# When the second latent block's experts are chosen: one head per 16 picks from pick 105, each with its own exponential, in place of one head per 8 picks from pick 52

## The chip, the core and the metric

The kernel runs on one core of one Trainium2 chip. The metric is device time in microseconds for one launch; lower is better. A core has TensorE (PE, matmuls), VectorE (DVE), ScalarE (ACT), GpSimd (POOL) and SyncE (SP), each with its own instruction stream; they wait for one another through semaphores. Transfers between HBM and on-chip memory are issued by POOL, ACT or SP and run on 16 DMA engines that all of them share.

## The reference

Two layers (`DEPTH = 2`) of a hybrid backbone work on 128 context tokens and 256 latent tokens, all rows of 1024 floats. A layer is a modulation, four token mixers, an output projection and a norm, and then the part that matters here, a retrieval of experts (PEER):

```python
q = (x @ wq).reshape(T, PEER_HEADS, 2, PEER_KEY_DIM // 2)          # 8 heads, two halves
s1 = einsum('thd,nd->thn', q[:, :, 0], k1); s2 = ... q[:, :, 1], k2  # 128 scores each
v1, i1 = lax.top_k(s1, 16); v2, i2 = lax.top_k(s2, 16)
cand_s = v1[..., :, None] + v2[..., None, :]                        # 16 x 16 sums
top_s, pos = lax.top_k(cand_s, 16); idx = cand_i[pos]               # 16 experts per head
g = softmax(top_s)                                                  # over the 16 of a head
a = einsum('td,tkd->tk', x, u[idx])                                 # 128 rows of u per token
y = einsum('tk,tkd->td', g * gelu(a), v[idx])                       # 128 rows of v per token
```

So each token needs 8 heads x 16 experts = 128 rows of `u` and 128 rows of `v`, 4 KB each, at addresses that depend on the data.

## The kernel before

Tokens are cut into three blocks of 128: block 0 is the context, blocks 1 and 2 are the latent tokens. A layer has two stages: an even stage (block 0) and an odd stage (blocks 1 and 2, which share attention). Over the whole kernel the experts are worked off as one line of 6 x 128 = 768 picks: a pick is one expert for each of a block's 128 tokens. The order is layer 0 blocks 0, 1, 2 and then layer 1 blocks 0, 1, 2; `BASE = [0, 128, 384, 512, 768]` (L49) is the pick at which each stage's experts begin. So stage 1 holds picks 128 to 383 (its second block from 256 on), stage 3 picks 512 to 767 (its second block from 640 on).

For a pick n the engines do this:
- POOL gathers 128 rows of `u` (L423) into slot n mod 4 of `u_rows` and, four picks later, the 128 rows of `v` (L430) into slot n mod 4 of `v_rows`. A gather of `u` waits until the row slot is free (the dot of pick n - 4 is done) and, at every 16th pick, for the head's indices (`idx_ready`); a gather of `v` waits until TensorE has added pick n - 4. POOL does u(n), v(n - 4), u(n + 1), v(n - 3), ... in that fixed order.
- DVE multiplies the rows with the token and sums (`dot`, L982).
- Every four picks ACT takes the gelu of four dots (L701), DVE multiplies by the softmax weight (`weigh`, L990), and ACT makes four diagonal matrices (L707).
- PE adds diagonal x rows into the block's result (`add`, L1302).

All other work (projections, attention, norms, the choice of the experts themselves) is laid beside this line by hand. Every piece carries a due pick, and `Beside` emits it on its engine behind the line's own instruction of that pick. DVE's dots run six picks ahead of its due picks (`DOT_AHEAD = 6`, L54): a piece due at pick t stands behind the dot of pick t + 6.

Choosing a head's experts has two steps. `best_eight` and `next_eight` find the 16 best of each half from the scores in PSUM; for an odd stage they do so for both blocks at once, in `late(s)`, one head per 16 picks: head h from pick BASE + 16h - 22 on, with two 8-matmul groups of the query projection on PE (L1079, one 1 MB `q_tile` load per head). `pick` (L752 to L778) then makes the 16 x 16 sums of one block and one head, takes the best 16, and writes 16 indices; it comes in three chunks, due at three picks one after another. It also writes the scores less their maximum to `gw`; ACT takes the exponential (`weights_exp`, L528) and DVE divides by the sum (`shares`, L803). For the first block of a stage `late` calls `pick` for each head, and each head has its own exponential. For the second block `second(s)` calls it (s = 1 and 3).

When a block's 128 picks are done, `update` (L956) adds the result to the tokens and norms them. Stage 2's token mixer (layer 1, block 0) is laid over picks 262 to 348, that is over the second block of stage 1. Layer 1's modulation weights (24 tiles of 1 MB, `ring`) run over picks 134 to 254. Over the second block of stage 3, picks 640 to 767, nothing is laid but its own line and the update of block 1 at 640.

Of the kernel before, what the change touches and what calls it, by code (L numbers as in the profile page):

```python
# [22 lines left out]
HEADS = 8  # L23
# [25 lines left out]
BASE = [0, PICKS, 3 * PICKS, 4 * PICKS, 6 * PICKS]  # L49
# [36 lines left out]
PLANS = [Plan(s) for s in range(len(STAGES))]  # L86


def late_at(s, h):
    return BASE[s] + max(0, 16 * h - 22)  # L90


def projs_before(s):
# [18 lines left out]
def turn_of(l, b):  # L112
    return l * NB + b
# [57 lines left out]
def program(nc, ins, outs):  # L171
    with ExitStack() as ctx:
# [3 lines left out]
        def sem(name):  # L176
            return ctx.enter_context(nc.semaphore(name))
# [152 lines left out]
        gexp_in = sem("gexp_in")  # L330
# [110 lines left out]
        def _(act):  # L441
            st = Steps(act)
# [85 lines left out]
            def weights_exp(b, h):  # L528
                st.take(gexp_in)
                st.give(nc.scalar.activation(gw[:, b, h], gw[:, b, h], ACT.Exp), gexp_out)  # L530
# [139 lines left out]
            def late(s):  # L670

                for h in range(1, HEADS):
                    yield late_at(s, h) + 3
                    query(s, h)
                    yield late_at(s, h) + 10
                    weights_exp(PLANS[s].bs[0], h)

            def second(s):

                yield BASE[s] + 111  # L680
                weights_exp(PLANS[s].bs[1], slice(0, HEADS))

            def norms():

# [13 lines left out]
            def weigh(g):  # L698
# [4 lines left out]
                for m in range(GROUP):  # L703
                    n = g * GROUP + m
                    if n >= DIAGS:
# [3 lines left out]

            beside = Beside(modulation(0), modulation(1), *[mixer(s) for s in range(4)], *[late(s) for s in range(4)],  # L710
                            *[roots(s) for s in range(4)], roots_y(), second(1), second(3), norms(), results())
            beside.until(-1 - WEIGHT_AHEAD)
            for t in range(-WEIGHT_AHEAD, TOTAL):
# [10 lines left out]
        def _(dve):  # L724
            st = Steps(dve)
            V = nc.vector

            def step(ins_):
                st.step(ins_, dve_step)
# [19 lines left out]
                V.tensor_scalar(ada[:, SC1:SC1 + KC, :], ada[:, SC1:SC1 + KC, :], 1.0, None, ALU.add)  # L749
                st.step(V.tensor_scalar(ada[:, SC2:SC2 + KC, :], ada[:, SC2:SC2 + KC, :], 1.0, None, ALU.add), ada_ready)  # L750

            def pick(l, b, h, last):  # L752

                turn = turn_of(l, b)
                step(V.tensor_tensor(cand[:].rearrange("p (i j) -> p i j", i=TOPK),
                                     best[:, b, 0, h].unsqueeze(2).to_broadcast([P, TOPK, TOPK]),
                                     best[:, b, 1, h].unsqueeze(1).to_broadcast([P, TOPK, TOPK]), ALU.add))
                step(V.max(top[:, 0:8], cand[:]))
                V.max_index(pos[:, 0:8], top[:, 0:8], cand[:])
                step(V.match_replace(cand2[:], top[:, 0:8], cand[:], LOW))  # L760
                yield
                step(V.max(top[:, 8:16], cand2[:]))
                step(V.max_index(pos[:, 8:16], top[:, 8:16], cand2[:]))
                ins_ = V.tensor_tensor(gw[:, b, h], top[:], top[:, 0:1].to_broadcast([P, TOPK]), ALU.subtract)
                if last:
                    st.give(ins_, gexp_in)
                V.tensor_scalar(pos_ij[:, 0], pos[:], 4, None, ALU.logical_shift_right)
                V.tensor_scalar(pos_ij[:, 1], pos[:], 15, None, ALU.bitwise_and)
                step(V.tensor_copy(best_f[:], best_i[:, b, :, h]))
                step(V.tensor_copy(pos_f[:], pos_ij[:]))  # L770
                yield
                full = [P, 2, TOPK, TOPK]
                step(V.tensor_tensor(same[:], pos_f[:].unsqueeze(3).to_broadcast(full),
                                     iota16[:].unsqueeze(1).unsqueeze(1).to_broadcast(full), ALU.is_equal))
                step(V.tensor_tensor(same[:], same[:], best_f[:].unsqueeze(2).to_broadcast(full), ALU.mult))
                step(V.tensor_reduce(found[:], same[:], AX_X, ALU.add))
                step(V.tensor_scalar(idx_f[:], found[:, 0], float(N_KEYS), float(l * EXPERTS), ALU.mult, ALU.add))
                st.step(V.tensor_tensor(idx[:, b, h * TOPK:(h + 1) * TOPK], idx_f[:], found[:, 1], ALU.add), idx_ready[turn % 2])  # L778

            def best_eight(s, h):  # L780

                st.take(top_ready)
                sides = [(2 * i + half, b, half, ps_q[:, (2 * i + half) * P:(2 * i + half + 1) * P])
                         for i, b in enumerate(PLANS[s].bs) for half in range(2)]
                for i, b, half, scores in sides:
                    ins_ = V.max(best[:, b, half, h, 0:8], scores)
                step(ins_)
                for i, b, half, scores in sides:
                    V.max_index(best_i[:, b, half, h, 0:8], best[:, b, half, h, 0:8], scores)
                    ins_ = V.match_replace(scr[:, i, :], best[:, b, half, h, 0:8], scores, LOW)  # L790
                st.step(ins_, top_free)

            def next_eight(s, h):

                sides = [(2 * i + half, b, half) for i, b in enumerate(PLANS[s].bs) for half in range(2)]
                for i, b, half in sides:
                    ins_ = V.max(best[:, b, half, h, 8:16], scr[:, i, :])
                step(ins_)
                for i, b, half in sides:
                    ins_ = V.max_index(best_i[:, b, half, h, 8:16], best[:, b, half, h, 8:16], scr[:, i, :])  # L800
                step(ins_)

            def shares(b, h):  # L803

                st.take(gexp_out)
                n = h.stop - h.start
                step(V.tensor_reduce(gsum[:, h], gw[:, b, h], AX_X, ALU.add))
                step(V.reciprocal(gsum[:, h], gsum[:, h]))
                step(V.tensor_tensor(gw[:, b, h], gw[:, b, h],
                                     gsum[:, h].unsqueeze(2).to_broadcast([P, n, TOPK]), ALU.mult))  # L810

            def mixer(s):
                T_ = PLANS[s]
                l, c, bs, nb, w = T_.l, T_.c, T_.bs, T_.nb, T_.width
# [32 lines left out]
                ins_ = V.tensor_tensor(qk[:, 0:nb], qk[:, 0:nb], qk_g[:].unsqueeze(1).to_broadcast([P, nb, 6, HD]), ALU.mult)  # L847
                if c == 0:
                    st.step(ins_, k_out_ready)
                else:  # L850
                    step(ins_)
                    for i in range(nb):
# [5 lines left out]
                        for e in range(4):  # L858
                            ins_ = V.tensor_tensor(r5[:, :, e, :], s5[:, :, e ^ 1, :],
                                                   sin[:, e, :].unsqueeze(1).to_broadcast([P, 6, 16]), ALU.mult)  # L860
# [38 lines left out]
                for i, b in enumerate(bs):  # L899
# [9 lines left out]
                    ins_ = V.tensor_tensor(x[:, b, :], x[:, b, :], ln_b[:], ALU.add)  # L909
# [8 lines left out]
                best_eight(s, 0)  # L918
                yield T_.query + 5
                next_eight(s, 0)  # L920
                parts = pick(l, bs[0], 0, True)
                for i in range(3):
                    yield T_.query + 6 + i
                    next(parts, None)
# [5 lines left out]
            def late(s):  # L930
                T_ = PLANS[s]
                for h in range(1, HEADS):
                    at_ = late_at(s, h)
                    yield at_ + 5
                    best_eight(s, h)
                    yield at_ + 6
                    next_eight(s, h)
                    parts = pick(T_.l, T_.bs[0], h, True)
                    for i in range(3):
                        yield at_ + 7 + i  # L940
                        next(parts, None)
                    yield at_ + 11
                    shares(T_.bs[0], slice(h, h + 1))

            def second(s):

                T_ = PLANS[s]
                for h in range(HEADS):
                    parts = pick(T_.l, T_.bs[1], h, h == HEADS - 1)
                    for i in range(3):  # L950
                        yield BASE[s] + 52 + 8 * h + i
                        next(parts, None)
                yield BASE[s] + 112
                shares(T_.bs[1], slice(0, HEADS))

            def update(turn):  # L956

# [28 lines left out]
            def weigh(g):  # L986
# [5 lines left out]

            dve.wait_ge(iota_ready, 1)
            beside = Beside(*[update(t) for t in range(TURNS)], modulation(0), modulation(1), *[mixer(s) for s in range(4)],
                            *[late(s) for s in range(4)], second(1), second(3))
            beside.until(-1 - DOT_AHEAD)
            for t in range(-DOT_AHEAD, TOTAL):
# [397 lines left out]
```

## Time and profile before

| what | value |
|---|---|
| time, median of 3 runs (lowest to highest) | 2770.77 us (2766.0 to 2777.85) |
| the profiled execution: own time | 2775.02 us |
| the profiled execution: span of the trace | 2773.2 us |
| mean granted TensorE clock | 0.95 |
| PE, DVE, ACT, POOL busy, share of the span | 82%, 56%, 24%, 61% |
| bytes moved | 954.02 MB, mean 344 GB/s |

The profile is of one execution; the times in its rows are microseconds from the start of its span. A busy share is a mean over the whole span, while the stages have different limits, so the rows below are taken by stretches of 16 picks. A stretch begins where the dot of its first pick begins.

### The profile page before, as it was taken

Reading aid. Unit: us, or ns where it says so; the run is one execution under the profiler, and the core shown is the slowest. Engines: PE = TensorE matmul, PEld = TensorE weight load, DVE = VectorE, ACT = ScalarE, POOL = GpSimd, SP = SyncE. Lnnn points to the kernel's source line nnn. Section 1 sums busy time; section 2 is a strip of 40 time slices with the busy share of each in tenths; the row PEclk is TensorE's granted clock in tenths of the full one; section 3 lists DMA queues with packets and bytes.
Section 4 is the critical chain, followed back from the end, with each engine's and each line's share of the span. In section 5 each row is a group of like instructions: output and inputs, shape, how many; then the busy total and the mean of one; then the engine's idle time right before and its main releaser. Section 6 shows DMA issues by size and latency. Waiting matters only on the chain.

```text
span 2773.2 us, 24064 instructions
## 1 busy us (share of the span) xinstructions
PE 2286.2 (82%) x7331; PEld 1163.9 (42%) x7331; DVE 1555.4 (56%) x3936; ACT 654.2 (24%) x1647; POOL 1683.8 (61%) x1584
## 2 busy tenths in 40 slices
PE   5984899997789999787877799999778787667776
PEld 2463565563344444244333366556433343222222
DVE  0015656666555787543555565576656788554444
ACT  0132324423121121121512232451312211111111
POOL 3003566665566567767776655566657777777775
PEclk8977999998999999999999999999989999999999
DMA  8835899999899999999999989899979999999997
GB/s 272 258 117 200 323 376 335 333 331 345 333 356 374 372 396 394 385 356 399 387 393 376 360 333 383 304 326 327 324 288 380 369 358 349 352 365 406 407 407 311
DMA packets 359635, 954.02 MB, mean 344 GB/s; under 512 B 29248, under 2 KB 159572, under 8 KB 359380
## 3 DMA queue, kind: packets, MB, share of 16 engines
q0 software_dynamic: 222976, 810.02, 77.4%
q1 hardware_dynamic: 99348, 98.60, 10.7%
q10 hardware_dynamic: 37184, 43.86, 4.6%
q8 instruction: 61, 1.00, 0.1%
q14 instruction: 66, 0.54, 0.1%
HBM read 950.00 MB, written 2.36 MB: 343 GB/s over the span
## 4 chain that ended last, share of the span: by engine, by line
PE 42%; DMA 22%; POOL 16%; DVE 10%; issue 8%; ACT 2%; ACTq 0%; SPq 0%; DVEq 0%; POOLq 0%
PE ps L1302 20%; DMA v_rows<-in_peer_v_dram,idx 10%; DMA u_rows<-in_peer_u_dram,idx 10%; POOL v_rows L430 9%; POOL u_rows L423 8%; PE ps L1062 5%; PE ps L1079 5%; DVE u_rows L982 4%; PE ps L1128 3%; PE ps L1257 3%; DMA ring<-in_w_ada_dram 1%; PE ps L1123 1%; PE ps L1203 1%; PE ps L1229 1%; ACT diag L707 1%
## 5 line engine op out<-in xcount | busy, mean ns | idle before, releaser
L1302 PE MATMUL ps<-v_rows,diag 128*128 128x512 f32 x3072 | 1506.2, 625 | 376.0 <-DMA v_rows<-in_peer_v_dram,idx 191.4
L982 DVE CUSTOM_DVE_ANT_0 u_rows<-u_rows,h 128x1024 f32<-128x1024 f32 x768 | 941.3, 1227 | 913.9 <-DMA u_rows<-in_peer_u_dram,idx 906.6
L430 POOL DMA_INDIRECT v_rows<-in_peer_v_dram,idx x768 | 828.1, 1078 | 556.6 <-PE ps L1302 383.4
L423 POOL DMA_INDIRECT u_rows<-in_peer_u_dram,idx x768 | 832.7, 1084 | 514.0 <-DVE idx L778 274.9
L1302 PEld LDWEIGHTS ps<-v_rows,diag 128*128 128x128 f32 x3072 | 564.6, 197 | 1145.6 <-issue 860.0
L707 ACT ACTIVATE diag<-ident,weight 128x128 f32<-128x128 f32 x768 | 245.3, 390 | 510.6 <-DVE weight L990 507.3
L701 ACT ACTIVATE gelu<-dots 128x4 f32<-128x4 f32 x192 | 39.4, 205 | 897.5 <-DVE dots L982 892.1
L1062 PE MATMUL ps<-ring,silu_c 128*2 128x256 f32 x768 | 182.0, 392 | 22.1 <-DMA ring<-in_w_ada_dram 21.7
L1079 PE MATMUL ps<-hT,q_tile 128*128 128x128 f32 (+1 forms) x1024 | 182.4, 333 | 0.0
L1079 PEld LDWEIGHTS ps<-hT,q_tile 128*128 128x128 f32 x1024 | 162.5, 196 | 36.2 <-issue 23.5
L1062 PEld LDWEIGHTS ps<-ring,silu_c 128*2 128x2 f32 x768 | 63.1, 87 | 137.4 <-issue 39.2
L1128 PE MATMUL ps<-ring,hT 128*128 128x256 f32 x480 | 112.3, 390 | 3.5 <-ACTq L516 3.5
L1128 PEld LDWEIGHTS ps<-ring,hT 128*128 128x128 f32 x480 | 94.5, 197 | 28.8 <-issue 16.7
L701 ACT ACT_TABLE_LOAD x67 | 86.0, 1283 | 39.4 <-DVE dots L982 16.6
L1257 PE MATMUL ps<-ring,hT 128*128 128x256 f32 x384 | 88.5, 386 | 0.5 <-issue 0.5
L1257 PEld LDWEIGHTS ps<-ring,hT 128*128 128x128 f32 x384 | 74.6, 195 | 19.5 <-issue 10.3
L741 DVE RECIPROCAL rstd<-rstd 128x1 f32<-128x1 f32 x18 | 2.9, 160 | 116.4 <-ACT rstd L485 115.9
L982 DVE DVE_READ_ACCUMULATOR2_ANT dots<- 128x1 f32 x768 | 63.4, 83 | 0.0
L474 ACT COPY ada_row<-ps 2x256 f32<-2x256 f32 x48 | 17.1, 357 | 166.6 <-PE ps L1062 166.5
L522 ACT COPY qT<-ps 128x256 f32<-128x256 f32 (+1 forms) x32 | 15.3, 477 | 156.4 <-PE ps L1079 156.3
L1031 PE MATMUL ps<-ident,h 128*128 128x128 f32 x96 | 17.0, 334 | 36.5 <-issue 23.8
L1123 PE MATMUL ps<-hT,ring 128*128 128x128 f32 (+1 forms) x256 | 44.0, 327 | 0.0
(174 smaller groups left out, 1429.1 us busy)
## 6 DMA issues: line engine op xcount, KB each, us to landing
ring<-in_w_ada_dram SPq DMA_DIRECT2D x48, 1024.0 KB, 12.1
q_tile<-in_peer_wq_dram ACTq DMA_DIRECT2D x32, 1024.0 KB, 12.0
ring<-in_w_in_dram SPq DMA_DIRECT2D x28, 1024.0 KB, 14.3
ring<-in_w_out_dram SPq DMA_DIRECT2D x16, 1024.0 KB, 12.9
u_rows<-in_peer_u_dram,idx POOLq DMA_INDIRECT x768, 6.6
v_rows<-in_peer_v_dram,idx POOLq DMA_INDIRECT x768, 6.6
ln_g<-in_ln_g_dram ACTq DMA_DIRECT2D x6, 512.0 KB, 7.5
ln_b<-in_ln_b_dram ACTq DMA_DIRECT2D x6, 512.0 KB, 10.2
```

The costliest lines, as they stand in the source:

```text
L423: nc.gpsimd.indirect_dma_start(u_rows[:, n % SLOTS, :], None, table_u, bass.IndirectOffsetOnAxis(idx[:, turn % NB, k:k + 1], 0)).then_inc( ...
L430: nc.gpsimd.indirect_dma_start(v_rows[:, n % SLOTS, :], None, table_v, bass.IndirectOffsetOnAxis(idx[:, turn % NB, k:k + 1], 0)).then_inc( ...
L701: nc.scalar.activation(gelu[:, g % 2, :], dots[:, g % 2, :], ACT.Gelu).then_inc(gelu_ready, 1)
L707: nc.scalar.activation(diag[:, n % DIAGS, :], ident[:], ACT.Copy, scale=weight[:, g % 2, m:m + 1]).then_inc(diag_ready, 1)
L982: V.tensor_tensor_reduce(out=u_rows[:, n % SLOTS, :], in0=u_rows[:, n % SLOTS, :], in1=h2[:, turn % NB, :], scale=1.0, scalar=0.0, op0=ALU ...
L1062: ins_ = M.matmul(ps_proj[i % 2][0:2, 0:WT], silu_c[:, :, k], w[:, k, :], start=(k == 0), stop=(k == KC - 1))
L1079: ins_ = M.matmul(ps_q[:, half * T_.width:(half + 1) * T_.width], q_tile[:, k, half * P:(half + 1) * P], hT[:, k, T_.lo:T_.hi], start=(k = ...
L1123: ins_ = M.matmul(to[:, 0:w], wt[:, k, i * P:(i + 1) * P], hT[:, k, T_.lo:T_.hi], start=(k == 0), stop=(k == KC - 1))
L1128: ins_ = M.matmul(to[:, 0:WT], hT[:, k, b * P:(b + 1) * P], wt[:, k, :], start=(k == 0), stop=(k == KC - 1))
L1203: ins_ = M.matmul(ps_sc[n % 2][:, 0:keys_n], q[64 * r:64 * r + 64, cq, i * P:(i + 1) * P], keys[64 * r:64 * r + 64, 0:keys_n], start=True, ...
L1257: ins_ = M.matmul(ps_sc[k_ % 2][:, 0:WT], mixT[:, k, b * P:(b + 1) * P], wt[:, k, :], start=(k == 0), stop=(k == KC - 1))
L1302: ins_ = M.matmul(ps_y[:, half * 512:(half + 1) * 512], diag[:, n % DIAGS, :], v_rows[:, n % SLOTS, half * 512:(half + 1) * 512], start=(n ...
```

## The change

For each head h of the second block the three chunks of `pick` move from BASE + 52 + 8h + (0, 1, 2) to BASE + 105 + 16h + (0, 1, 2). The one exponential over all eight heads at BASE + 111 becomes eight, each three picks after its head's first chunk, and the one `shares` over eight heads at BASE + 112 becomes eight, one pick after the exponential. This happens in stages 1 and 3. The argument `last` of `pick` falls away: every head now tells ACT that its scores are there.

```diff
+def second_at(s, h):
+    return BASE[s] + 105 + 16 * h
...
             def second(s):
 
-                yield BASE[s] + 111
-                weights_exp(PLANS[s].bs[1], slice(0, HEADS))
+                for h in range(HEADS):
+                    yield second_at(s, h) + 3
+                    weights_exp(PLANS[s].bs[1], h)
...
-            def pick(l, b, h, last):
+            def pick(l, b, h):
...
                 ins_ = V.tensor_tensor(gw[:, b, h], top[:], top[:, 0:1].to_broadcast([P, TOPK]), ALU.subtract)
-                if last:
-                    st.give(ins_, gexp_in)
+                st.give(ins_, gexp_in)
...
                 for h in range(HEADS):
-                    parts = pick(T_.l, T_.bs[1], h, h == HEADS - 1)
+                    parts = pick(T_.l, T_.bs[1], h)
                     for i in range(3):
-                        yield BASE[s] + 52 + 8 * h + i
+                        yield second_at(s, h) + i
                         next(parts, None)
-                yield BASE[s] + 112
-                shares(T_.bs[1], slice(0, HEADS))
+                    yield second_at(s, h) + 4
+                    shares(T_.bs[1], slice(h, h + 1))
```

## Rows read from the trace of the kernel before

**Rows 1.** The page's chain that ended last: shares of the span.

```profile
PE 42%; DMA 22%; POOL 16%; DVE 10%; issue 8%; ACT 2%; ACTq 0%; SPq 0%; DVEq 0%; POOLq 0%
```

**Rows 2.** Stretches of 16 picks, stage 3, dots 528 on; busy by engine, clock, DMA.

```profile
core 0: us, PE busy (x) PEld busy (x) DVE busy (x) ACT busy (x) POOL busy (x), PEclk, DMA share, GB/s
2071.40:2120.20 48.80, 39.20 (x95) 18.80 (x96) 31.23 (x93) 12.07 (x27) 35.81 (x34) 0.86 0.99 369
2120.20:2167.60 47.40, 38.45 (x109) 18.87 (x108) 30.90 (x91) 9.30 (x24) 35.72 (x33) 1.00 1.01 381
2167.60:2213.70 46.10, 34.60 (x90) 16.22 (x89) 36.39 (x109) 9.30 (x24) 33.62 (x30) 0.96 0.98 376
2213.70:2266.00 52.30, 41.92 (x112) 21.24 (x111) 41.96 (x129) 9.30 (x24) 36.58 (x34) 0.93 0.95 348
...
2313.70:2364.20 50.50, 39.47 (x109) 20.02 (x108) 41.94 (x129) 9.49 (x25) 35.70 (x33) 0.97 0.93 333
...
2464.40:2505.40 41.00, 31.44 (x65) 10.86 (x64) 20.04 (x37) 5.93 (x20) 31.25 (x33) 1.00 1.03 410
...
2671.20:2712.10 40.90, 31.38 (x65) 10.86 (x64) 20.03 (x36) 5.93 (x20) 30.94 (x33) 1.00 1.03 409
```

**Rows 3.** The same view, stages 1 and 2: dots 144, 160, 192, 224, 288, 304.

```profile
772.30:827.20 54.90, 46.62 (x145) 20.32 (x144) 31.27 (x94) 12.94 (x30) 36.82 (x35) 0.97 1.03 388
827.20:882.80 55.60, 51.38 (x168) 24.16 (x165) 30.80 (x91) 10.28 (x27) 35.67 (x32) 0.97 1.02 383
...
937.90:995.50 57.60, 55.14 (x187) 27.52 (x187) 42.23 (x129) 10.27 (x27) 35.75 (x35) 1.00 0.99 367
...
1050.20:1103.50 53.30, 49.55 (x165) 21.91 (x164) 41.84 (x128) 10.27 (x27) 37.42 (x32) 1.00 1.04 392
...
1263.50:1315.50 52.00, 40.91 (x135) 21.91 (x135) 20.06 (x36) 8.56 (x27) 38.15 (x32) 1.00 1.04 399
1315.50:1356.50 41.00, 36.83 (x109) 15.76 (x108) 22.61 (x49) 18.64 (x47) 30.47 (x32) 1.00 1.02 408
```

**Rows 4.** Timeline of DVE: dots 551 and 556 around a first-block head.

```profile
2143.56 1.22 DVE L982 CUSTOM_DVE_ANT_0 u_rows<-u_rows,h 128x1024 f32<-128x1024 f32 x1
...
2156.50 1.22 DVE L982 CUSTOM_DVE_ANT_0 u_rows<-u_rows,h 128x1024 f32<-128x1024 f32 x1 [0.41 <-DMA u_rows<-in_peer_u_dram,idx]
```

**Rows 5.** The same view: dots 360 and 364 around head 0 of stage 2.

```profile
1483.95 1.23 DVE L982 CUSTOM_DVE_ANT_0 u_rows<-u_rows,h 128x1024 f32<-128x1024 f32 x1 [0.98 <-DMA u_rows<-in_peer_u_dram,idx]
...
1495.08 1.23 DVE L982 CUSTOM_DVE_ANT_0 u_rows<-u_rows,h 128x1024 f32<-128x1024 f32 x1 [0.29 <-DMA u_rows<-in_peer_u_dram,idx]
```

**Rows 6.** The same view: dots around head 7 of stage 3's second block, and behind.

```profile
2372.45 1.22 DVE L982 CUSTOM_DVE_ANT_0 u_rows<-u_rows,h 128x1024 f32<-128x1024 f32 x1 [2.30 <-DMA u_rows<-in_peer_u_dram,idx]
...
2385.61 1.23 DVE L982 CUSTOM_DVE_ANT_0 u_rows<-u_rows,h 128x1024 f32<-128x1024 f32 x1 [1.83 <-DMA u_rows<-in_peer_u_dram,idx]
...
2399.55 1.23 DVE L982 CUSTOM_DVE_ANT_0 u_rows<-u_rows,h 128x1024 f32<-128x1024 f32 x1 [1.33 <-DMA u_rows<-in_peer_u_dram,idx]
...
2430.09 1.23 DVE L982 CUSTOM_DVE_ANT_0 u_rows<-u_rows,h 128x1024 f32<-128x1024 f32 x1 [1.72 <-DMA u_rows<-in_peer_u_dram,idx]
```

**Rows 7.** Timeline of POOL and DVE: three gathers against the dots.

```profile
2372.51 1.98 POOL L423 DMA_INDIRECT u_rows<-in_peer_u_dram,idx  x1 [0.30 <-issue]
...
2519.13 0.94 POOL L423 DMA_INDIRECT u_rows<-in_peer_u_dram,idx  x1 [0.30 <-issue]
2519.35 1.23 DVE L982 CUSTOM_DVE_ANT_0 u_rows<-u_rows,h 128x1024 f32<-128x1024 f32 x1 [1.25 <-DMA u_rows<-in_peer_u_dram,idx]
...
2524.25 0.94 POOL L430 DMA_INDIRECT v_rows<-in_peer_v_dram,idx  x1 [0.30 <-issue]
```

**Rows 8.** Line L530, the softmax exponential: durations (min/median/max), and who waited for it.

```profile
L530 ACT ACTIVATE gw<-gw x34: 215/216/310, 245.6 to 2382.7; 128x16 f32<-128x16 f32 x32, 128x128 f32<-128x128 f32 x2
L530 ACT ACT_TABLE_LOAD  x30: 1283/1283/1283, 240.3 to 2381.4; - x30
...
  DVE gsum L807: 0.5, 1
```

More of the change, by code:

```diff
@@ L920, in mixer @@
                 next_eight(s, 0)
-                parts = pick(l, bs[0], 0, True)
+                parts = pick(l, bs[0], 0)
                 for i in range(3):
@@ L937, in late @@
                     next_eight(s, h)
-                    parts = pick(T_.l, T_.bs[0], h, True)
+                    parts = pick(T_.l, T_.bs[0], h)
                     for i in range(3):
```

## Prediction, made before the changed kernel was run

> **What bounds the kernel now.** I read three views in this order. First the chain that ended last [rows 1]: PE, DMA, POOL and DVE all have a share and none has half. So no engine bounds the whole kernel; it is a loop (gather, dot, gelu, weight, diagonal, add, next gather) whose links take turns, and the question has to be put stretch by stretch. Second, the busy times of stretches of 16 picks. Where the line of picks runs alone, dots 656 to 751 of stage 3, six stretches take about 41.0 us each, 2.56 us a pick, with the DMA engines full (share 1.03, 409 to 410 GB/s) and DVE busy for 20.0 us of 41; the first and the last of the six stand in [rows 2]. That is the fast pace that any disturbance must be held against. Where stage 3 also chooses for its first block (dots 528 to 559) a stretch takes 48.8 and 47.4 us, and with two second-block heads more (dots 576 to 623) it takes 52.3 and 50.5 us in its first and last of three, with DVE up from 31 to 42 us and the DMA rate down from 381 to 348 and 333 GB/s [rows 2]. Over the same part of stage 1 the modulation tiles stream too: 54.9 and 55.6 us without second-block heads, 57.6 and 53.3 us with two of them, at DMA shares of 0.99 to 1.04 [rows 3]. Third, the timelines of DVE and POOL around single heads, for what one head costs.
>
> One more thing is to be seen in the timelines: POOL hardly waits in the fast pace, its gather takes 0.94 us with 0.30 us between two, so two gathers are 2.48 us of the 2.56 us of a pick [rows 7]. POOL is as full as the DMA engines there. And a gather that begins just behind the beginning of a dot lasts 1.98 us: the one at 2372.51 began 0.06 us behind the dot at 2372.45 [rows 6, 7], while the one that began 0.22 us ahead of the dot at 2519.35 lasted 0.94 us, and so did one 5 us later [rows 7]. So the phase between dots and gathers decides whether POOL keeps up.
>
> **The change part by part.** A piece due at pick t stands behind dot t + 6. So in stage 3 the heads' first chunks leave dots 570, 578, ... 626 and go to dots 623, 639, ... 735; in stage 1 they leave 186 to 242 and go to 239, 255, ... 351. The new head 0 stands within three dots of the old head 7 in both stages, so in each stage seven heads move and one stays.
>
> *What a head is.* Two heads more raise DVE's busy time of a stretch from 31.2 to 42.0 us, so 5.4 us a head [rows 2]. In the fast pace DVE idles 21 us in each stretch, so the sum of its work fits; what can hurt is that three chunks stand behind three dots in a row and hold the later dots up.
>
> *Taken away in stage 3.* The three stretches from dot 576 to 624 took 150.5 us (2213.70 to 2364.20). At the mean of the two stretches without second-block heads, 48.1 us, they take 144.3: 6.2 us gained. Bounds: nothing gained on one side; on the other, 46.1 us as in the stretch of dots 560 to 575 [rows 2], 12.2 us gained. I take 6.2.
>
> *Put in, stage 3.* Seven heads stand alone on the fast pace. What one costs there the trace shows three times, each time dots in a row against 2.56 us a dot. A first-block head at the same place in the group of four as the new ones: five dots in 12.94 us (2143.56 to 2156.50), 0.1 us over 12.8 [rows 4]. Head 0 of stage 2: four dots in 11.13 us, 0.9 over 10.25 [rows 5]. Head 7 of the second block, already outside the first block's choosing: four dots in 13.16 us, 2.9 over [rows 6]. The last has the likest surroundings, the first the likest phase: its chunks stand behind dots 3, 0, 1 of the group, so that only one of them is ahead of the weighing. I take the mean, 1.3 us; bounds 0.1 and 2.9 us, and more if a slow pace stays behind (rival 1). Seven heads: +9.1 us.
>
> *Stage 1.* Taken away: the three stretches from 937.90 to 1103.50 took 165.6 us, three at the mean of the two without such heads (55.25) take 165.75: nothing gained, at most the 2.4 us of the one slow stretch [rows 3]. Put in: heads at dots 271, 287 and 335 fall where weight tiles of stage 2 keep the DMA engines full (share 1.04, 399 GB/s, in the stretch of dot 288) and DVE is busy for 20 us of 52 [rows 3]; the transfers in line cover a late dot: 0. The head at 255 stands beside the update of block 1, where the adds pause anyway: 0. Those at 303, 319 and 351 fall on or beside the fast pace (41.0 us, 408 GB/s, dots 304 to 319 [rows 3]): three times 1.3, +3.9 us. Without the cover all seven would cost 9.1.
>
> *Exponentials and sums.* ACT issues 14 more exponentials of 0.22 us, each with at most two table loads of 1.28 us, one there and one back to gelu: 2.8 us a head [rows 8]. Cover: in the fast pace ACT is busy for 5.9 us of 41 [rows 2], and between an exponential, which follows the weighing of a group, and the next gelu lie three dots, 7.7 us. If that cover went, the gelu of one group would come up to 2.8 us late. Each exponential waits for the head's second chunk, due two picks earlier; behind it on ACT stands only that gelu. Each `shares` waits for the exponential; behind it stand the dots. Of 34 such waits one was felt, for 0.5 us [rows 8]. `shares` is three small instructions where three larger ones stood once: within the head's 1.3 us. Cost 0.
>
> *Deadlines.* Head h's indices are written behind dot BASE + 113 + 16h; POOL asks for them after dot BASE + 124 + 16h. Eleven picks at 2.56 us, 28 us: POOL does not wait. No DMA issue moves on any queue.
>
> By the Trainium skill, "SBUF — State Buffer", section "SBUF: two separate sides", VectorE with two SBUF inputs and GpSimd share a port pair as an exclusive lock, and whoever starts first holds it for its whole instruction. The trace agrees for the gather at 2372.51 (1.98 us); that a gather holds up a dot it does not show: the dot at 2519.35 began inside a gather and kept its 1.23 us. By the rule in full, each late dot would also lose up to one gather, 0.94 us, three a head: 2.8 us, and the seven heads would cost 20 us in stage 3 instead of 9.1, rival 1 in half.
>
> *Sum.* Stage 3: -6.2 + 9.1 = +2.9. Stage 1: 0 + 3.9 = +3.9. Together +6.8 us. The profiled execution took 2775.0 us (span 2773.2, 1.8 around it), so 2781.8 by its own time; it lay 4.2 above the median of 2770.8, so against the median 2777.6, say 2778.
>
> **The rivals.**
> (1) Slower: a head leaves the slow phase behind. Behind old head 7, with nothing chosen, the eleven picks from the dot at 2399.55 to the one at 2430.09 took 30.5 us, 2.78 us each, 0.2 over the fast pace, and only the update behind them ended it [rows 6]. If every one of the seven new heads of stage 3 costs 2.9 us and then 0.2 us for the 13 picks to the next, that is 5.5 us a head, 38 us; with 12 us for four heads of stage 1 and 6 gained: +44, 2815. If half of them do, about 2793. It decides once the mean price of a head passes 2.0 us (seven heads and three: 20 - 6 = 14 us). For it: the old head 7. Against: rows 4 and 5, where the next dots catch up.
> (2) Faster: the relief is larger. Without the two extra heads the stretches could come down to the bytes: 41.0 us of rows and one 1 MB tile more (2.6 us), 43.6 us, so 150.5 - 131 = 19.5 us gained, and with 0.1 us a head some 2752. Against: dots 528 to 559, without such heads, did not [rows 2].
> (3) It does nothing that can be seen: DVE's work is hidden at both places, 2771. For it: stage 1 shows no price at all for two heads a stretch [rows 3].
>
> **How the numbers follow.** A measurement tells about 0.5% from no change, 13.9 us: below 2756.9 is faster, above 2784.6 slower. Forecast with its near neighbours 0.32, rival 3 0.24, rival 1 in full or half 0.31, rival 2 0.13. The first two are no change: 0.56. Lowest sum of the bounds: -12.2 - 2.4 + 0.7, 2757; highest without rival 1: 0 + 10 x 2.9 = +29, 2800. The range takes half and most of rival 1 in and leaves the end of either out: 2758 to 2810.
>
> **What would show it.** Right: dots 576 to 623 near 48 us a stretch with DVE at 31 us; dots 656 to 751 near 42.3 us a stretch with DVE near 26 us and POOL's gathers of `u` and `v` seldom over 0.94 us; no wait of POOL for indices there. Wrong: stretches of 44 us and more behind dot 656 (rival 1), stretches near 44 us ahead of dot 624 (rival 2), adds that wait for diagonals behind a table load, or steps of stage 2's attention that are late by a chunk.

## Result: 0.4% slower, and the profile after

Median 2785.05 us (20 runs, 2768.79 to 2799.27) against 2776.27 us for the kernel before on the same occasions (20 runs, 2764.04 to 2783.8). The ratio is 1.0037, 95% interval 1.002 to 1.0055: slower, clear of noise, and within the 0.5% that the prediction counts as no change. The time lies inside the stated range, 7 us above the predicted 2778; by the ratio the change costs 10.3 us where the sum said 6.8. The profiled execution after has a span of 2778.6 us, 5.4 more than before.

Stretches of 16 picks after, the view of rows 2 and 3; first two of stage 1 (dots 192 and 304), then stage 3 (dots 576, 608, 624, 656, 688, 736):

```profile
core 0: us, PE busy (x) PEld busy (x) DVE busy (x) ACT busy (x) POOL busy (x), PEclk, DMA share, GB/s
940.20:994.00 53.80, 51.58 (x176) 25.69 (x175) 30.94 (x90) 10.17 (x27) 36.77 (x34) 1.00 1.04 393
...
1314.80:1358.00 43.20, 37.19 (x109) 15.88 (x108) 28.61 (x71) 21.44 (x50) 32.45 (x32) 1.00 1.00 390
2216.80:2265.10 48.30, 37.42 (x102) 17.44 (x102) 30.87 (x91) 9.30 (x24) 36.28 (x32) 1.00 0.98 365
...
2312.70:2359.70 47.00, 38.82 (x96) 18.00 (x95) 32.44 (x96) 9.30 (x24) 36.04 (x33) 0.93 0.96 357
2359.70:2403.10 43.40, 31.71 (x66) 10.84 (x64) 25.88 (x59) 8.72 (x23) 33.15 (x34) 1.00 1.01 398
2453.60:2497.10 43.50, 31.52 (x65) 10.87 (x64) 25.85 (x58) 8.71 (x23) 33.74 (x33) 1.00 0.99 377
...
2539.60:2583.10 43.50, 31.12 (x65) 10.86 (x64) 25.84 (x58) 8.72 (x23) 34.05 (x32) 1.00 1.00 378
...
2673.00:2715.70 42.70, 30.61 (x63) 10.84 (x64) 24.27 (x53) 8.72 (x23) 33.24 (x32) 1.00 1.00 390
```

Against [rows 2] the trade is plain. Dots 576 to 623, which lost two heads a stretch, take 142.9 us (2216.8 to 2359.7) for 150.5. Dots 624 to 639, where head 0 now stands in place of head 7, take 43.4 for 49.2 (the first line below). And dots 656 to 751, which got a head a stretch, take 262.1 for 247.7: +14.4 us, 2.4 a head. DVE is far from full there (25.9 us of 43.5); what grew beside it is POOL, from about 31 to 34 us a stretch.

The stretch of dot 624 before; then the six stretches from dot 656 on as one window, before and after:

```profile
2364.20:2413.40 49.20, 33.15 (x70) 11.71 (x69) 26.09 (x58) 8.80 (x23) 38.83 (x35) 1.00 0.96 350
```

```profile
2464.40:2712.10 247.70, 188.41 (x385) 65.14 (x384) 120.23 (x216) 35.59 (x120) 188.29 (x193) 1.00 1.02 407
```

```profile
2453.60:2715.70 262.10, 190.75 (x384) 66.72 (x384) 153.56 (x343) 52.29 (x138) 203.85 (x192) 0.98 1.00 383
```

And what POOL waited for in the six, before and then after (in all, times, longest; "issue" is time in which nothing seen holds it):

```profile
POOL v_rows L430 <- issue: 29.4, 95, 0.5
POOL u_rows L423 <- issue: 29.3, 96, 0.3
POOL v_rows L430 <- PE ps L1302: 1.1, 2, 0.8
```

```profile
POOL u_rows L427 <- issue: 29.3, 96, 0.3
POOL v_rows L434 <- issue: 19.8, 65, 0.3
POOL v_rows L434 <- PE ps L1306: 9.5, 31, 0.3
```

After, no wait is longer than 0.3 us. So POOL goes from gather to gather without a stop, 203.85 us of gathers and 58.6 us of such gaps, together 262.4: the stretch lasts as long as POOL's own instructions. Before it was the same at a shorter length, 188.29 us of gathers and 59.8 us of gaps. The gathers themselves became longer, by 15.6 us over the six stretches, and the time by 14.4: of some 192 gathers 35 last over 1.2 us, where before there were 3.

Why longer is to be seen behind one head (head 4, whose first chunk stands behind the dot at 2536.61). Timeline of DVE and POOL after; the first, third and last dot lines are dots 687, 692 and 703:

```profile
2536.61 1.23 DVE L986 CUSTOM_DVE_ANT_0 u_rows<-u_rows,h 128x1024 f32<-128x1024 f32 x1 [1.33 <-DMA u_rows<-in_peer_u_dram,idx]
...
2539.59 1.22 DVE L986 CUSTOM_DVE_ANT_0 u_rows<-u_rows,h 128x1024 f32<-128x1024 f32 x1
...
2549.47 1.23 DVE L986 CUSTOM_DVE_ANT_0 u_rows<-u_rows,h 128x1024 f32<-128x1024 f32 x1 [0.32 <-DMA u_rows<-in_peer_u_dram,idx]
2549.88 1.63 POOL L434 DMA_INDIRECT v_rows<-in_peer_v_dram,idx  x1 [0.30 <-issue]
...
2560.48 1.23 DVE L986 CUSTOM_DVE_ANT_0 u_rows<-u_rows,h 128x1024 f32<-128x1024 f32 x1 [1.83 <-DMA u_rows<-in_peer_u_dram,idx]
2561.00 1.52 POOL L434 DMA_INDIRECT v_rows<-in_peer_v_dram,idx  x1 [0.30 <-PE ps L1306]
...
2568.92 1.23 DVE L986 CUSTOM_DVE_ANT_0 u_rows<-u_rows,h 128x1024 f32<-128x1024 f32 x1 [1.96 <-DMA u_rows<-in_peer_u_dram,idx]
2569.31 1.65 POOL L434 DMA_INDIRECT v_rows<-in_peer_v_dram,idx  x1 [0.30 <-PE ps L1306]
...
2580.13 1.22 DVE L986 CUSTOM_DVE_ANT_0 u_rows<-u_rows,h 128x1024 f32<-128x1024 f32 x1 [1.68 <-DMA u_rows<-in_peer_u_dram,idx]
```

This head itself costs nothing: five dots in 12.86 us (2536.61 to 2549.47), 0.1 over the fast pace, as in [rows 4]. The price comes behind it: eleven dots in 30.66 us (2549.47 to 2580.13), 2.5 over 28.2, with nothing chosen. Summed over the six heads, and against the same dots before, the five dots at a head took 2.3 us more (80.7 for 78.4) and the eleven behind it 12.5 us more (181.8 for 169.3). Behind head 4 gathers begin 0.4 to 0.5 us behind a dot's beginning and last 1.5 to 1.65 us in place of 0.94. Each of the three shown ends 0.81 us behind the end of its dot. A long gather brings its rows, and those of the gathers behind it, late; a later dot is late in turn (2560.48 and 2568.92 waited 1.83 and 1.96 us for rows, where 1.33 is usual), and it holds the next gather. POOL fills 2.48 of the 2.56 us of a pick, so it has almost nothing with which to make up.

### The profile page after: what moved, and what is told of

Read it like the earlier page. It is cut to its first block, busy times and chain, and to the rows that moved or that the text cites. A ratio compares the mean times of both kernels' runs of the same rounds, so it can differ in the third digit from the quotient of the medians.

```text
span 2778.6 us, 24164 instructions
## 1 busy us (share of the span) xinstructions
PE 2268.8 (82%) x7331; PEld 1157.3 (42%) x7331; DVE 1558.2 (56%) x3978; ACT 690.6 (25%) x1687; POOL 1721.0 (62%) x1584
## 4 chain that ended last, share of the span: by engine, by line
PE 41%; DMA 21%; POOL 19%; DVE 8%; issue 8%; ACT 2%; SPq 0%; DVEq 0%; ACTq 0%
PE ps L1306 19%; DMA v_rows<-in_peer_v_dram,idx 10%; POOL v_rows L434 10%; POOL u_rows L427 10%; DMA u_rows<-in_peer_u_dram,idx 9%; PE ps L1066 5%; PE ps L1083 5%; DVE u_rows L986 3%; PE ps L1132 3%; PE ps L1261 3%; DMA ring<-in_w_ada_dram 1%; PE ps L1127 1%; PE ps L1207 1%; PE ps L1233 1%; PE ps L1221 1%
## 5 line engine op out<-in xcount | busy, mean ns | idle before, releaser
L1306 PE MATMUL ps<-v_rows,diag 128*128 128x512 f32 x3072 | 1490.4, 619 | 389.7 <-DMA v_rows<-in_peer_v_dram,idx 210.8
L427 POOL DMA_INDIRECT u_rows<-in_peer_u_dram,idx x768 | 861.0, 1121 | 510.3 <-DVE idx L782 273.0
L434 POOL DMA_INDIRECT v_rows<-in_peer_v_dram,idx x768 | 836.9, 1090 | 528.1 <-PE ps L1306 368.3
L1306 PEld LDWEIGHTS ps<-v_rows,diag 128*128 128x128 f32 x3072 | 557.0, 194 | 1151.9 <-issue 861.9
L1261 PEld LDWEIGHTS ps<-ring,hT 128*128 128x128 f32 x384 | 74.2, 194 | 19.6 <-issue 10.3
L478 ACT COPY ada_row<-ps 2x256 f32<-2x256 f32 x48 | 17.2, 358 | 165.7 <-PE ps L1066 165.7
```

What stands on the lines that cost most here:

```text
L427: nc.gpsimd.indirect_dma_start(u_rows[:, n % SLOTS, :], None, table_u, bass.IndirectOffsetOnAxis(idx[:, turn % NB, k:k + 1], 0)).then_inc( ...
L434: nc.gpsimd.indirect_dma_start(v_rows[:, n % SLOTS, :], None, table_v, bass.IndirectOffsetOnAxis(idx[:, turn % NB, k:k + 1], 0)).then_inc( ...
L1261: ins_ = M.matmul(ps_sc[k_ % 2][:, 0:WT], mixT[:, k, b * P:(b + 1) * P], wt[:, k, :], start=(k == 0), stop=(k == KC - 1))
L1306: ins_ = M.matmul(ps_y[:, half * 512:(half + 1) * 512], diag[:, n % DIAGS, :], v_rows[:, n % SLOTS, half * 512:(half + 1) * 512], start=(n ...
```

## The experiments

Theory A: the price is this, gathers held behind dots that a head's chunks made late. Rival B: the seven additional exponentials a stage and their table loads hold up gelu, diagonals and adds. Rival C: the mere amount of DVE work on the fast pace. A dot is called late if DVE comes to it from other work, without idling for its rows: of the 96 dots of the six stretches 21 are late after, none before. Line numbers differ a little between the kernels; "six stretches" are dots 656 to 751.

### One stage alone

```diff
 def second_at(s, h):
-    return BASE[s] + 105 + 16 * h
+    return BASE[s] + (105 + 16 * h if s == 3 else 52 + 8 * h)
```

with one exponential and one division in the unchanged stage, as before; the second kernel has `s == 1` there.

> Only stage 3 has the change; stage 1 chooses as before. By the two traces the change moved dots 560 to the end of stage 3 from 605.6 to 609.4 us, so +3.8 us; ratio to before 1.001 to 1.002. If the whole effect sat here, 1.0037. If the price of the heads on the fast pace were outweighed by the relief, as the low bound of the prediction has it, 0.998 or less.

> Only stage 1 has the change. By the two traces dots 176 to 399 went from 727.9 to 730.5 us: +2.6 us, ratio 1.001. The prediction's term for this stage was +3.9 us, 1.0014. If stage 1 gains, because dots 192 to 239 went from 165.6 to 161.9 us and the rest is chance, 0.999.

Measured: stage 3 alone 1.0026 (1.0009 to 1.0044), stage 1 alone 1.0013 (0.999 to 1.0036). So stage 3 has most of it, a little more than expected, stage 1 perhaps a little, not told from nothing; together 1.0039, near the 1.0037 of the whole change. The six stretches of stage 3, with the same program as after, take 258.1 us in the first kernel's profile, so the 14.4 us of the change's own profile is 10.4 here:

```profile
2458.00:2716.10 258.10, 188.16 (x384) 65.70 (x384) 153.40 (x343) 52.29 (x138) 199.36 (x193) 0.99 1.00 389
```

Stage 1 alone has a span of 2771.6 us in its profile, under before's 2773.2, while its median is above: single executions differ by more than this term.

### Without the exponentials

This kernel leaves out the second block's exponentials and the division by their sum; its weights for that block are raw differences.

```diff
             def second(s):
-                for h in range(HEADS):
-                    yield second_at(s, h) + 3
-                    weights_exp(PLANS[s].bs[1], h)
+                return
+                yield
```

> The changed kernel without the second block's exponentials and without the division by their sum (its weights stay the raw differences of the scores); heads at the same picks. Theory A, the price is paid by POOL, whose gathers are held behind dots that a head's chunks made late: no change against the changed kernel, dots 656 to 751 of stage 3 stay near 262 us (six stretches of 43.7 us), ratio to before 1.003 to 1.004. Rival B, the table loads hold up gelu, diagonals and adds: the six stretches fall to 250 us or less, ratio 0.999 or less.

Measured: 1.003 (1.0007 to 1.0054). The six stretches:

```profile
2446.10:2710.10 264.00, 189.44 (x386) 65.89 (x385) 151.11 (x325) 35.60 (x120) 204.95 (x192) 0.99 1.00 381
```

ACT is back at the 35.6 us of before, and the stretches stay at 264 us. Rival B falls: the exponentials cost nothing here. The changed kernel's own exponentials (line L534, in the view of rows 8) agree:

```profile
L534 ACT ACTIVATE gw<-gw x48: 215/216/217, 244.2 to 2677.0; 128x16 f32<-128x16 f32 x48
L534 ACT ACT_TABLE_LOAD  x43: 1283/1283/1283, 239.0 to 2675.7; - x43
...
  DVE gsum L811: 0.5, 1
```

Fourteen exponentials and thirteen loads to them more, and the division waited once for 0.5 us, as before.

### Small pieces

`pick` got four more places to yield at, so that a second-block head comes in seven pieces of 0.7 to 1.1 us at seven picks.

```diff
-                    parts = pick(T_.l, T_.bs[1], h)
-                    for i in range(3):
+                    parts = pick(T_.l, T_.bs[1], h, True)
+                    for i in range(7):
                         yield second_at(s, h) + i
                         next(parts, None)
-                    yield second_at(s, h) + 4
+                    yield second_at(s, h) + 8
                     shares(T_.bs[1], slice(h, h + 1))
...
                 step(V.max(top[:, 0:8], cand[:]))
+                if fine:
+                    yield
...
                 step(V.max_index(pos[:, 8:16], top[:, 8:16], cand2[:]))
+                if fine:
+                    yield
```

and two more between the three steps over `same`; the exponential is due at + 6.

> The changed kernel with each second-block head's choice cut into seven pieces of 0.7 to 1.1 us at seven picks one after another, in place of three chunks of 1.7 to 2.4 us; its exponential six picks and its division eight picks behind the first piece. All the work is there. Theory A: no piece is longer than DVE's idle time of 1.3 us between two dots, so dots start on time, POOL's gathers keep their phase (0.94 us, excess under 0.1), the six stretches from dot 656 on take 41 to 42 us each (250 us in all, 12 less), and with the relief ahead of dot 640 kept the ratio to before is 0.994 to 0.998. Rival B or C (table loads, or the mere amount of DVE work): the stretches stay at 43.7 us, ratio 1.003 to 1.005.

Measured: 0.9972 (0.9952 to 0.9991), faster than before by 0.28%, where the same work in three chunks was slower by 0.37%. The six stretches, and gathers against dots inside a head:

```profile
2451.10:2699.90 248.80, 188.25 (x385) 65.06 (x384) 152.32 (x347) 52.30 (x138) 190.06 (x193) 1.00 1.02 406
```

```profile
2537.02 0.93 POOL L434 DMA_INDIRECT v_rows<-in_peer_v_dram,idx  x1 [0.30 <-issue]
2537.24 1.23 DVE L994 CUSTOM_DVE_ANT_0 u_rows<-u_rows,h 128x1024 f32<-128x1024 f32 x1 [0.47 <-DMA u_rows<-in_peer_u_dram,idx]
...
2539.59 0.94 POOL L434 DMA_INDIRECT v_rows<-in_peer_v_dram,idx  x1 [0.30 <-issue]
2539.79 1.23 DVE L994 CUSTOM_DVE_ANT_0 u_rows<-u_rows,h 128x1024 f32<-128x1024 f32 x1 [0.44 <-DMA u_rows<-in_peer_u_dram,idx]
```

DVE and ACT do what they do after (152 and 52 us), the same heads at nearly the same picks; the stretches fall from 262.1 to 248.8 us and POOL's gathers from 203.85 to 190.06. DVE still idles 0.4 us ahead of each of these dots, so each begins on the landing of its rows, 0.2 us behind the beginning of a gather, not ahead of it. Over the six stretches no dot is late (21 after), and 6 gathers last over 1.2 us (35 after). Theory A gave 250 us, and the ratio that it gave. The amount of work in one head (rival C) is not what costs.

This holds for stage 3. Stage 1 did not gain by small pieces: dots 240 to 383 take 453.6 us in this profile, 449.0 after and 445.0 before. What they lose there theory A does not explain.

### Twice the work, in small pieces

After a head's seven pieces its steps are done once more in the next seven picks, without a use of their results (in stage 1 those of head 7 meet the choice of stage 2's first head and spoil its scratch, so the context output differs).

```diff
+                    again = repeat(T_.bs[1], h)
+                    for i in range(7):
+                        yield second_at(s, h) + 7 + i
+                        next(again, None)
+                        if i == 1:
+                            shares(T_.bs[1], slice(h, h + 1))
```

> e4_fine with the choosing of each second-block head done a second time, in the seven picks behind the first, without its results being used: DVE's work for these heads is doubled, no piece is longer. Theory A: the six stretches from dot 656 on stay near 250 us (at most 254) with DVE near 31 us of 41 in each, ratio as e4_fine's, 0.996 to 0.999. Rival C, the amount of DVE work is what costs: the six stretches go to 262 us or more, ratio 1.002 or more.

Measured: 1.0015 (0.9993 to 1.0037), above the expected 0.999. The profile is of the fastest of its 12 runs; its six stretches take 256.1 us, between the 254 of theory A and the 262 of rival C. Four of the six stretches, the first, second, third and sixth:

```profile
2446.00:2491.80 45.80, 31.48 (x65) 10.84 (x64) 30.24 (x75) 8.71 (x23) 35.91 (x33) 1.00 0.99 372
2491.80:2536.60 44.80, 32.74 (x65) 11.51 (x64) 30.52 (x75) 8.71 (x23) 34.87 (x33) 0.96 1.00 377
2536.60:2577.80 41.20, 31.15 (x65) 10.84 (x64) 30.27 (x75) 8.72 (x23) 31.36 (x33) 1.00 1.03 409
...
2660.90:2702.00 41.10, 31.61 (x66) 10.84 (x65) 29.71 (x73) 8.72 (x23) 31.34 (x33) 1.00 1.02 399
```

This speaks for neither in full. With DVE at 30 us of 41 the fast pace can hold, so the amount as such does not slow a stretch. But the first two stretches run at a slow pace, 45 us, with the same work as the third, and again it is POOL that is longer (35.9 against 31.4). There are two paces with the same work, and one changes into the other without a cause in the program's order. Late dots do not tell them apart: here one dot a head is late, behind a division and a repeated piece, in the slow stretches as in the fast ones.

### Two picks later

The changed kernel with `second_at` at 107, so that all three chunks stand between two weighings; then the same with the division two picks further behind; then the small pieces at 107.

```diff
 def second_at(s, h):
-    return BASE[s] + 105 + 16 * h
+    return BASE[s] + 107 + 16 * h
```

> The changed kernel with every second-block head two picks later (from pick 107): all three chunks now stand between two weighings instead of one of them ahead of a weighing and two behind. Theory A (late dots and POOL's phase): the three dots are as late as before, the six stretches from dot 656 on stay at 258 to 266 us, ratio 1.002 to 1.006. The reason given in the prediction for a low price (only one chunk ahead of the weighing) would make it dearer: weight and diagonals 2.5 us late in every head, 270 us or more, ratio above 1.007.

> e6_phase2 (three chunks a head from pick 107) with the division by the sum two picks later, so that DVE no longer waits for the exponential (9.3 us in six waits in e6_phase2's six stretches). If that wait was what made e6_phase2 dearer than the changed kernel: the six stretches at 258 to 266 us, ratio 1.002 to 1.006. If it was the weighing behind three chunks: 268 us or more, ratio 1.006 or more.

> e4_fine with every head two picks later (from pick 107). No piece is longer than DVE's idle time, so no dot is late whatever the place: the six stretches from dot 656 on near 250 us (at most 254), ratio 0.995 to 0.999, as e4_fine. If the place of a head against the weighings has a price of its own, as e6_phase2's 271 us could be read: 258 us or more, ratio 1.001 or more.

Measured: 1.007 (1.0049 to 1.0091), 1.0065 (1.0039 to 1.009) and 0.9991 (0.9965 to 1.0017). The six stretches of the first; then, in the view of waits over them, the one that it has and the changed kernel has not (in all, times, longest); then the six stretches of the second:

```profile
2447.40:2718.30 270.90, 193.41 (x386) 68.70 (x384) 155.81 (x349) 52.30 (x138) 207.56 (x193) 0.97 0.98 373
```

```profile
DVE gsum L811 <- ACT gw L534: 9.3, 6, 1.7
```

```profile
2450.50:2719.40 268.90, 194.08 (x385) 69.69 (x384) 155.43 (x349) 52.29 (x138) 205.79 (x192) 0.96 0.99 374
```

The wait for the exponential is gone in the second and the stretches are 2 us shorter, not 9: that wait was not the cause. So the place of three long chunks against the weighing has a price of its own, about 1.1 us a head (268.9 against 262.1 over six; 0.8 to 1.8 against the 258.1 to 264.0 us of the three profiles with such chunks at 105). That is the reason which the prediction gave for a low price of the changed kernel's heads; theory A alone, which said that the place is indifferent, was too simple.

The third missed. No dot is late in its six stretches, and they take 259.2 us all the same, where theory A allowed 254 and the rival asked for 258. Its ratio lies between the two. Against the same place with long chunks it is still a gain, 0.9991 for 1.007. Its profile, the second slowest of its 12 runs by span (2786.1 us; 2764.5 to 2787.3), has dots 656 to 671, 704 to 719 and 720 to 735 so:

```profile
2466.30:2510.50 44.20, 32.27 (x67) 11.24 (x67) 25.67 (x58) 8.72 (x23) 34.51 (x32) 1.00 0.99 377
2599.00:2642.80 43.80, 33.05 (x65) 11.30 (x64) 25.75 (x59) 8.72 (x23) 33.75 (x34) 0.96 1.01 387
2642.80:2683.70 40.90, 31.33 (x65) 10.84 (x64) 25.67 (x58) 8.72 (x23) 31.15 (x33) 1.00 1.03 410
```

A slow pace is there from the update at 640 on, lasts four stretches, and gives way to the fast one with the same work in line. Where nothing is chosen (before, stage 1 alone, and the kernel of the next section) all six stretches ran fast in each profile. So long chunks bring the slow pace in with nearly every head; small ones do so less often, but a slow pace that is already there can last among them. So a late dot is one way into the slow pace and not the only one.

### The old heads one pick later

The kernel before with 53 + 8h in place of 52 + 8h (exponential and division one pick later too).

> The kernel before with its second-block heads one pick later (53 + 8h), so that their chunks stand to the weighings as those of the changed kernel do. If the slow pace behind the old head 7 came from its place in the group of four, dots 624 to 639 of stage 3 fall from 49.3 us to 43 to 45 and dots 576 to 623 from 150 to 145, ratio 0.995 to 0.998. If that head was slow because of what lies ahead of it (the last first-block heads) or by chance: 47 to 50 us, ratio 0.999 to 1.001.

Measured: 0.9993 (0.9978 to 1.0009). Dots 576 to 623 and 624 to 639:

```profile
2218.00:2373.40 155.40, 121.36 (x315) 59.08 (x313) 125.46 (x386) 28.09 (x73) 102.50 (x99) 0.93 0.93 341
2373.40:2417.20 43.80, 32.59 (x63) 12.02 (x64) 26.16 (x58) 8.80 (x23) 32.34 (x31) 0.92 0.98 374
```

Half right. Old head 7, moved by one pick, no longer leaves the 49.2 us of before but 43.8; that speaks for its place in the group of four. It is one profile against two, for the kernel with stage 1 alone changed, which has head 7 at the old place, took 46.7. But the three stretches ahead did not get shorter, they took 155.4 us for 150.5, and nothing is left in the median.

### Versions that beat both

Small pieces in both stages with one head per 8 picks from 105 in stage 1; and small pieces in stage 3 alone, stage 1 as before.

```diff
 def second_at(s, h):
-    return BASE[s] + 105 + 16 * h
+    return BASE[s] + 105 + (8 if s == 1 else 16) * h
```

> Seven small pieces a head as in e4_fine; stage 3 at one head per 16 picks from 105, stage 1 at one head per 8 picks from 105, so that it is through at dot 304, ahead of the fast stretches beside stage 2's attention. Theory A (a head costs only where a piece makes a dot late on the fast pace): stage 3 keeps the 16 us that e4_fine took from it, stage 1 no longer loses the 5 us of dots 304 to 384 (41 and 45 us again for dots 304 to 335), and the ratio is below e4_fine's 0.9972: 0.992 to 0.996. If stage 1's loss is chance or the amount of DVE work there, the ratio stays at 0.997.

> Stage 1 chooses as in the kernel before; stage 3 as in e4_fine (seven small pieces a head, one head per 16 picks from 105). By the traces stage 3 takes 567 us from dot 560 to the end in place of 583, and stage 1 is as before: 10 to 16 us less, ratio 0.994 to 0.997. If e4_fine's gain came from stage 1 as well, 0.998 or more.

Measured: 0.996 (0.9936 to 0.9985) and 0.9948 (0.9925 to 0.9971). The six stretches of the second:

```profile
2451.50:2699.80 248.30, 188.31 (x385) 65.03 (x384) 152.93 (x347) 52.31 (x138) 189.59 (x193) 1.00 1.02 406
```

Both beat the kernel before and the change; the second is the best measured, 0.5% under before. The gain is stage 3's. The three versions with small pieces from 105 are not told from one another, so what stage 1 should do stays open. The first did not bring dots 304 to 335 all the way back (87.2 us; before 85.9, changed 89.6), though its second-block heads are through ahead of dot 304. Its six stretches of stage 3 take 252.7 us: none of their dots is late, and yet dots 688 to 703 take 44.7, behind two stretches of 41.3 and 41.6.

## Why the prediction was right, and by which steps

**What bounds the stretch.** Right, and more strictly than said: on the fast pace it is POOL, whose gathers and gaps fill the whole stretch.

**Relief in stage 3**, 6.2 us: measured 7.6 in the two traces (150.5 to 142.9); 141.7 to 143.4 in the other profiles with the heads gone from there, and 152.5 and 155.4 in the two others that keep them, so the relief is nearer 10. The step was right, its size on the low side. DVE came down to 31 us, as foreseen.

**Head 0 for head 7**, counted as one that stays: wrong by 5.8 us (49.2 to 43.4; 3.3 against the other profile with the old place). They stand three dots apart, but in another place of the group of four; the old heads moved by one pick make it likely that this place made the slow stretch.

**The heads on the fast pace in stage 3**, 9.1 us for seven: mis-sized. Head 1, beside the update, cost nothing (51.0 and 50.5 us); the six others cost 14.4, 2.4 each where 1.3 was taken (1.7 in the profile with stage 3 alone changed, 2.7 in the one without the exponentials). The failing step is the mean over three rows. [Rows 4] were nearly right for the head itself, 0.1 us there and 0.4 in the mean of the six; the other 2 us a head come behind it as a slow pace, which the prediction had seen [rows 6] and left to rival 1. The mechanism of rival 1 is what happened, at 2.4 us a head in place of its 5.5, and weighed against a relief of 13 us in stage 3 that it had put at 6. An error of 5 us (14.4 for 9.1) and one of 7 us (13 for 6) so stood against each other. That the sum came out near is luck.

**Stage 1**: 3.9 us put in, measured 4.0 from dot 240 to 383 (445.0 to 449.0), of which 2.2 in dots 304 to 319; taken away 3.6 (165.6 to 162.0) where nothing was expected and 2.4 was the bound. In the eight other profiles with heads gone from dots 192 to 239 these take 162.2 to 164.5 us, in the three others where heads stay there 163.4 to 165.7. The means are 163.0 and 164.8, the ranges overlap; about 2 us may be real. The loss in dots 304 to 319 is no surer: they also took 44.4 us, for 41.0 before and 43.3 after, in the version whose second-block heads are through ahead of dot 304. Alone, the stage gives 1.0013, not told from 1.

**Exponentials, divisions, deadlines**, 0: right, shown by the kernel without exponentials; POOL's waits for indices are 273.0 us in six waits, 274.9 before, of which one wait at the start of the kernel is 223.5 (224.9 before), and none lies behind 2200 us.

**The lock.** The Trainium skill, "SBUF — State Buffer", "SBUF: two separate sides", has the shared port pair held by whoever starts first, VectorE with two SBUF inputs only against a GpSimd operation that reads SBUF, as the gather reads its indices. For a gather behind a dot the traces agree: 1.52 to 1.65 us, ending 0.81 us behind the dot. For a dot inside a gather they do not: 518 of the 768 dots after begin inside one, and the longest of these takes 1.25 us. So the price that the rule gave in full, 20 us, did not come; the 14.4 us measured came through gathers alone.

**Rival 2** (relief down to 131 us) and rival 3 (nothing) are out by these runs. The parts named here, as the two traces have them, add up to +1 us (-7.6 - 5.8 - 0.4 + 14.4 - 3.6 + 4.0); the two spans differ by 5.4, and the ratio says +10 (5 to 15). Between single executions of one kernel lie 30 us, so where the rest lies is not settled. Nor is it settled what sets off or ends a slow pace where no piece is long.

## What to carry to other kernels

Where a queue of gathers issues almost without a gap, slack on the engine beside it is not room for work in any size: cut that work to pieces shorter than the engine's idle time between two dots, here under 1.3 us, and the same work changed from +0.37% to -0.28% (two picks later from +0.70% to -0.09%). Price a moved step by what the loop does in the picks behind it, not only by the picks in which it stands. And compare places only at the same phase of the loop's groups: two picks' shift was worth about 1 us a head.

## What the runs showed of the hardware that was not expected

An indirect gather that begins early in the two-input dot ends 0.81 us behind the dot's end, so it lasts up to about 2 us in place of 0.94; a dot that begins inside a gather is not held (1.25 us at most in the trace after). And the loop has two paces with the same instructions, about 41 and about 44 to 46 us for 16 picks, that last for tens of picks: at 30 us of DVE work both were seen in one execution.
